# Norms: GpSimd adds squared tiles in pairs, and TensorE sums the pairs with ones

## The reference

```python
def layer_norm(x, g, b):
    mu = jnp.mean(xf, axis=-1, keepdims=True)
    var = jnp.mean(jnp.square(xf - mu), axis=-1, keepdims=True)
    y = (xf - mu) * lax.rsqrt(var + LN_EPS) * g + b

# and, without centring,
y = x * lax.rsqrt(jnp.mean(x * x, axis=-1, keepdims=True) + eps) * w
```

## Time and profile before

| what | value |
|---|---|
| median of 3 runs | 4329.05 us (4323.47 to 4330.01) |
| the profiled execution | 4340.69 us, its span 4338.9 us |
| TensorE busy | 3790.5 us, 87% of the span, 19109 matmuls |
| VectorE busy | 2528.5 us, 58% |
| ScalarE busy | 1207.0 us, 28% |
| GpSimd busy | 348.2 us, 8%, 276 instructions |
| granted TensorE clock, mean | 0.93 |
| sums of squares (L153) on TensorE | 176 matmul records |
| squares (L166) on ScalarE | 88 |

### The profile page before, as it was taken

The page is one execution under the profiler, slowest core; times in us unless marked ns, Lnnn a source line. Parts: engine busy times, 40 slices in busy tenths (PEclk is TensorE's granted clock), DMA queues, the critical chain, the costliest instruction groups (busy, mean ns, idle before and its releaser), DMA issues. The chain is left out here.

```text
span 4338.9 us, 51551 instructions
## 1 busy us (share of the span) xinstructions
PE 3790.5 (87%) x19109; PEld 3261.0 (75%) x19109; DVE 2528.5 (58%) x4080; ACT 1207.0 (28%) x2101; POOL 348.2 (8%) x276
## 2 busy tenths in 40 slices
PE   7998977799986988889999979999877879779998
PEld 6876764478755787689999979999856848566876
DVE  4544778454434563369999867777643436654433
ACT  1101122121012232233578833333221122412300
POOL 0000011000000020002212212222100000000000
PEclk9999978799998989999999989999988979889999
DMA  3222710222211001238889889998612101021232
GB/s 140 97 71 82 255 60 1 95 74 96 73 64 58 29 1 40 87 119 271 293 291 330 307 302 329 324 336 314 220 58 73 51 33 67 1 78 68 87 104 71
DMA packets 198386, 590.94 MB, mean 136 GB/s; under 512 B 22448, under 2 KB 80688, under 8 KB 196016
## 3 DMA queue, kind: packets, MB, share of 16 engines
q1 hardware_dynamic: 161344, 454.38, 30.3%
q0 software_dynamic: 36864, 134.23, 8.7%
HBM read 536.11 MB, written 52.43 MB: 136 GB/s over the span
## 5 line engine op out<-in xcount | busy, mean ns | idle before, releaser
L350 DVE CAST w_hi<-w_ring 128x1024 fp32r<-128x1024 f32 (+1 forms) x336 | 238.5, 710 | 644.0 <-PE banks L315 495.8
L71 DVE TENSOR_TENSOR w_lo<-w_ring,w_hi 128x1024 fp32r<-128x1024 f32 (+1 forms) x336 | 424.5, 1263 | 11.5
L315 PE MATMUL banks<-x_hi,w_hi 128*128 128x512 f32 x896 | 355.8, 397 | 46.9 <-DVE x_lo L71 46.8
L2385 PE MATMUL out_ps<-w_hi,v_hi 128*128 128x384 f32 x1024 | 349.2, 341 | 45.5 <-DVE w_lo L71 45.5
L2085 PE MATMUL up_ps<-h_hi,u_hi 128*128 128x384 f32 x1024 | 351.4, 343 | 21.2 <-DVE u_lo L71 21.2
L315 PE MATMUL banks<-x_lo,w_hi 128*128 128x512 f32 x896 | 354.4, 396 | 0.0
L315 PE MATMUL banks<-x_hi,w_lo 128*128 128x512 f32 x896 | 354.2, 395 | 0.0
L2385 PE MATMUL out_ps<-w_hi,v_lo 128*128 128x384 f32 x1024 | 347.6, 339 | 0.0
L2385 PE MATMUL out_ps<-w_lo,v_hi 128*128 128x384 f32 x1024 | 347.6, 339 | 0.0
L2085 PE MATMUL up_ps<-h_lo,u_hi 128*128 128x384 f32 x1024 | 343.8, 336 | 0.0
L2085 PE MATMUL up_ps<-h_hi,u_lo 128*128 128x384 f32 x1024 | 343.6, 336 | 0.0
(11 more groups left out here) (532 smaller groups left out, 7812.0 us busy)
## 6 DMA issues: line engine op xcount, KB each, us to landing
expert_tiles<-peer_u SPq DMA_DIRECT2D x128, 512.0 KB
expert_tiles<-peer_v SPq DMA_DIRECT2D x128, 512.0 KB
w_ring<-w_in SPq DMA_DIRECT2D x104, 512.0 KB, 3.6
w_ring<-ffn_up SPq DMA_DIRECT2D x88, 512.0 KB, 3.5
w_ring<-w_ff SPq DMA_DIRECT2D x64, 512.0 KB, 3.8
ada_ring<-w_ada SPq DMA_DIRECT2D x48, 512.0 KB, 5.2
peer_acts<-act_ring SPq DMA_DIRECT2D x128, 192.0 KB
peer_gates<-staging SPq DMA_DIRECT2D x12, 2048.0 KB
```

The source lines that it names most:

```text
L71: return nc.vector.tensor_tensor(self.lo[at], value, self.hi[at].bitcast(F32), ALU.subtract)
L315: last = nc.tensor.matmul(banks[:, j, s, 0:n], a[:, u % 2, k, :], b[:, g * kg + k, x_from + c:x_from + c + n], start=(g == 0 and k == 0 an ...
L350: nc.vector.tensor_copy(w_parts.hi[:, u % 2], ring[:, u % slots]).then_inc(hi_ready, 1)
L2385: last = nc.tensor.matmul(out_ps[:, b, P:T], a[:, n % 2, b * P:b * P + P], r[:, n % 2, :], start=(n == 0 and part == 0), stop=(n == NKEYS ...
```

## The change

Where a norm has at least four slots, GpSimd adds the squares of tiles 2i and 2i+1 into the slot of the former, as soon as both are there. TensorE waits for that sum and multiplies it with ones, so a norm of eight tiles has four summed tiles, and one of four tiles has two. ScalarE's wait for a free slot is now for the summed pair: squares 4 and 5 wait for pair 0, squares 6 and 7 for pair 1. The norm with two slots stays as it was. All stage classes get a GpSimd part, `run` and `linear` play it, and each of these norms takes one more semaphore. One clearing of semaphores, with its barrier, is added in the second block, ahead of the projection "out2".

```diff
--- before.py
+++ after.py
@@ -87,6 +87,9 @@
     def tensor(self, pe):
         pass
 
+    def gpsimd(self, pool):
+        pass
+
     def scalar(self, act):
         for k in range(self.kb):
             self.p.nc.scalar.activation(self.parts.hi[:, k, :], self.src[:, k, :], ACT.Copy).then_inc(self.hi_ready, 1)
@@ -115,6 +118,9 @@
         self.sq = p.sb(ctx, "squares", [P, 4, width])[:] if squares is None else squares
         self.rstd = p.sb(ctx, "rstd", [P, width])[:] if rstd is None else rstd
         self.slots = self.sq.shape[1]
+        self.paired = self.slots >= 4
+        self.sums_of = kb // 2 if self.paired else kb
+        (self.pair_ready,) = p.sems(ctx, "pair_ready") if self.paired else (None,)
         self.dst = dst
         self.eps_col = p.sb(ctx, "eps_col", [P, 1])
         self.sums = p.ps(ctx, "sums", [P, 2 if center else 1, halves, 512])
@@ -147,12 +153,24 @@
                     last = nc.tensor.matmul(self.sums[:, 0, j, 0:n], self.p.ones, self.src[:, k, c:c + n],
                                             start=(k == 0), stop=(k == kb - 1))
             last.then_inc(self.mean_ready, 1)
-        for k in range(kb):
-            pe.wait_ge(self.sq_ready, k + 1)
+        for i in range(self.sums_of):
+            if self.paired:
+                pe.wait_ge(self.pair_ready, i + 1)
+            else:
+                pe.wait_ge(self.sq_ready, i + 1)
+            at = (2 * i if self.paired else i) % self.slots
             for j, (c, n) in enumerate(self.spans):
                 last = nc.tensor.matmul(self.sums[:, 1 if self.center else 0, j, 0:n], self.p.ones,
-                                        self.sq[:, k % self.slots, c:c + n], start=(k == 0), stop=(k == kb - 1))
+                                        self.sq[:, at, c:c + n], start=(i == 0), stop=(i == self.sums_of - 1))
             last.then_inc(self.sq_used, 1)
+
+    def gpsimd(self, pool):
+        if self.paired:
+            for i in range(self.sums_of):
+                at = 2 * i % self.slots
+                pool.wait_ge(self.sq_ready, 2 * i + 2)
+                self.p.nc.gpsimd.tensor_tensor(self.sq[:, at, :], self.sq[:, at, :], self.sq[:, at + 1, :], ALU.add) \
+                    .then_inc(self.pair_ready, 1)
 
     def scalar(self, act):
         nc, kb, center = self.p.nc, self.kb, self.center
@@ -162,11 +180,11 @@
             else:
                 self.source_ready(act, k)
             if k >= self.slots:
-                act.wait_ge(self.sq_used, k - self.slots + 1)
+                act.wait_ge(self.sq_used, (k - self.slots) // 2 + 1 if self.paired else k - self.slots + 1)
             nc.scalar.activation(self.sq[:, k % self.slots, :], (self.dst if center else self.src)[:, k, :], ACT.Square) \
                 .then_inc(self.sq_ready, 1)
         act.wait_ge(self.eps_set, 1)
-        act.wait_ge(self.sq_used, kb)
+        act.wait_ge(self.sq_used, self.sums_of)
         nc.scalar.activation(self.halved(self.rstd), self.total(1 if center else 0), ACT.Sqrt, bias=self.eps_col[:],
                              scale=1.0 / (kb * P)).then_inc(self.rms_ready, 1)
         for k in range(kb):
@@ -214,6 +232,9 @@
     def __init__(self, landed, count):
         self.landed, self.count = landed, count
 
+    def gpsimd(self, pool):
+        pool.wait_ge(self.landed, 16 * self.count)
+
     def tensor(self, pe):
         pe.wait_ge(self.landed, 16 * self.count)
 
@@ -238,6 +259,11 @@
         def _(act):
             for stage in stages:
                 stage.scalar(act)
+
+        @block.gpsimd
+        def _(pool):
+            for stage in stages:
+                stage.gpsimd(pool)
 
         @block.vector
         def _(dve):
@@ -297,6 +323,11 @@
                 with sp.Fori(0, bodies - 1) as i:
                     body(i, False)
             body(bodies - 1, True)
+
+        @block.gpsimd
+        def _(pool):
+            for stage in front:
+                stage.gpsimd(pool)
 
         @block.tensor
         def _(pe):
@@ -1124,6 +1155,7 @@
             mix = p.sb(c, "mix", [P, DB, T])
             mixer2(p, x, mix, ln3, gains[:, 0, :], sh1, gm_norm, o_norm)
             mix_parts = Parts(p, c, "mix", [P, DB, T])
+            p.clear_semaphores()
             linear(p, "out2", d["w_out2"], DB, DB, mix_parts, dve_out=residual_out(p, x, gt1),
                    stages=lambda c2: [Split(p, c2, mix, mix_parts, DB)])
         p.clear_semaphores()
```

## The result

The change makes the kernel slower: 4345.96 us in the median of 8 runs (4338.21 to 4353.44) against 4330.81 of the kernel before (8 runs, 4319.48 to 4337.83) on the same chip, ratio 1.0039 with a 95% interval of 1.0027 to 1.0052, so 12 to 23 us. The forecast was 4341 in a range of 4326 to 4355. The two profiled executions lie only 4.7 us apart, where the forecast had 4352.4 for the later one. Executions differ by more than that outside of the norms, so what follows compares the norms one by one and takes the total from the medians.

The account below looks back on a forecast made before the run. Eleven serial norm windows that nothing covers were taken as the bound, TensorE's matmuls setting the pace inside. 6.6 + 0.3 + 2.2 + 1.2 + 0.6 + 0.85 = 11.75 us on the 4329.05 median gave 4341, range 4326 to 4355.

Parts of the forecast that it names:

- The price of an add: GpSimd's addition of two tiles of squares takes 1.21 us, bounds 1.14 and 1.36.
- The schedule: Long norm, square 4 waiting for pair 0's sum: 8.6 us at full clock against 7.90 before, 11.1 at half.
- The clock, warm norms: Three norms formerly at full clock: a 3.3 us pause before the first sum lowers it, 10.1 us each, +6.6 in all.
- Cold norms: Five norms starting at half clock: full clock returns late or never, 10.6 us each, together +0.3, bounds -2.2 and +2.8.
- the meeting at 1750: GpSimd's adds 1 and 2 coincide with VectorE's weight splits, one waiting out the other: +1.2 us, bounds 0 and 2.4.
- Short norms: Two norms of four tiles: 5.6 us against 4.49, together +2.2, bounds +0.8 and +3.8.
- The narrow norm: Norm of the meta tokens' sixteen columns, at 3144: adds meet VectorE's splits, +0.6 us, bounds 0 to 2.
- The clearing: New barrier ahead of the second mixer's output projection delays its weight fetch: +0.85 us, bounds 0.3 and 1.4.
- The first rival: Full clock survives the 3.3 us pause in at least two of three warm norms: about +3.4 us, 4332; chance 0.3.
- the second: Rival: sums spaced by adds keep TensorE at half clock in every norm, +19 us, 4348; chance 0.2.

Follow-up runs that it names:

- the change once more: The changed kernel unaltered, run again for a second profile and more runs: 4347.59 us, ratio 1.0042 to the kernel before.
- clearing alone: The kernel before with only the added clearing of semaphores ahead of the second mixer's output projection: 4329.11 us, ratio 1.0008.
- fillers: The changed kernel with matmuls of constants, results overwritten, ahead of the first pair's sum in five norms: 4333.68 us, ratio 1.0021 to the kernel before.
- adds twice: The changed kernel with a second GpSimd addition of the same size behind each: 4378.65 us, ratio 1.0123 to the kernel before.
- eight slots: The changed kernel with eight slots in place of four for the squares in six long norms: 4331.03 us, ratio 1.0000 to the kernel before.
- sums one by one: The kernel before, with VectorE adding each square to the first in four norms and TensorE summing one tile: 4326.91 us, ratio 1.0001.
- keep warm: The kernel before, with matmuls of constants, results overwritten, ahead of the sums in four norms that start at half clock: 4320.69 us, ratio 0.9980.
- warm, pairs on VectorE: The kernel before with constant matmuls ahead of sums in five norms; in four, VectorE adds the pairs, with six slots: 4312.83 us, ratio 0.9960.

## Why the prediction held

The kernels can be put in one table. The middle column is the sum of the eleven windows less the 89.4 of before, with 1.4 us for the clearing where it is in; the last is what was timed.

| kernel | windows and clearing | as a ratio | measured ratio |
|---|---|---|---|
| the change | +12.6 | 1.0029 | 1.0039 |
| the change once more | +14.2 | 1.0033 | 1.0042 |
| clearing alone | +1.3 | 1.0003 | 1.0008 |
| fillers | +8.1 | 1.0019 | 1.0021 |
| adds twice | +54.4 | 1.0126 | 1.0123 |
| eight slots | +3.2 | 1.0007 | 1.0000 |
| sums one by one | -4.4 | 0.9990 | 1.0001 |
| keep warm | -10.7 | 0.9975 | 0.9980 |
| warm, pairs on VectorE | -17.3 | 0.9960 | 0.9960 |

Each measured ratio is within 0.11% of its windows, and each interval holds the ratio of the windows: from -17 to +54 us, what a norm gains or loses comes out in the time. Nothing covers a norm, which was the ground the forecast stood on.

Step by step, with the two profiles of the change:

- **The price of an add**: 1.21 us forecast from GpSimd's own rows, 1.27 measured. The ratio of 2 to VectorE of the Trainium skill (GPSIMD Engine Reference, section Engine selection) gave an estimate of 1.36; against VectorE's 0.69 us the measured ratio is 1.84. The page's advice, VectorE for such an add, fits the last experiment, which also had the slots and the warm clock.
- **The schedule**: 8.6 us at full clock forecast, 8.83 at 1.00 measured. The slot wait that it names (square 4 behind pair 0) is in the timeline, and eight slots take it away.
- **The clock, warm norms**: +6.6 forecast, +7.4 and +7.9 measured. The pause was 3.40 us (3.3 forecast). The size was right, the course in part luck. The forecast took half clock at first and full clock for the last pair, 10.1 us, and no warm norm did that. Two ran all sums at half clock (11.22 and 11.09, the 11.1 of the schedule), one none (8.83, its 8.6), and three began at full clock and fell during the second pair (10.36 to 10.65), a case that the forecast did not have. That the mean of the six, 10.5, lies near 10.1 is owed to the mixture of these cases and not to the one that was forecast.
- **Cold norms and the meeting at 1750**: +0.3 and +1.2 forecast, together -0.3 and +0.8 measured. Here the mixed case is found, if with two pairs at full clock at the end: 10.26, 10.08 and 10.19 us, and 11.12 where all stayed at half. Which norm came back varied between the profiles (3151 and 3172 had 11.01 and 10.94 in the second), so the forecast's middle holds for the group only. The meeting is there, at 0.7 and 1.0 us of adds instead of 1.2.
- **Short norms**: +2.2 forecast, +3.5 in both profiles. The step that failed in size is the middle of 4.9 and 6.4: both short norms came out nearer to the cold end or past it, with 5.96 to 6.54.
- **The narrow norm**: +0.6 forecast, +0.7 measured.
- **The clearing**: +0.85 forecast, +1.36 measured, its upper bound. The comparison took another place, which has 1.34 us with a clearing where this one has 1.85 and 1.88; why isn't shown. The same place with and without the line gives the price.

In sum 11.75 forecast, 12.6 and 14.2 found in the profiles, 15 and 17 in the medians. The terms that were too small (warm norms, short norms, clearing: 2.6 and 3.1 us) and those that were too large (cold norms and meeting: 1.8 and 0.7 us) cancel in part. The bounds as they were added give 4327 to 4354, and the range was stated 1 us wider on each side; that decides nothing here. The first rival, a warm clock, happened in one of six warm windows, and not in two of three, as it would have had to; the second, half clock everywhere, in none of the two profiles as a whole.

## What to carry to other kernels

Taking work off the busiest engine can cost time where that work lies in a serial passage: count the chain from the first input to the last consumer, with every hand-off and every buffer that must come free, not the engine's sum. Combining tiles two by two also doubles the grain at which buffers come free, so it wants more slots. And look at what a pause does to TensorE's clock before and after it: here the clock was worth 3 us in a passage of 8, more than the whole idea of the pairs.

## What the runs showed of the hardware that was not expected

- The length of TensorE's pause alone did not decide the clock: after 3.40 us ahead of the first sum the window at 1269 had 1.00 (8.83 us) in one execution of the same kernel and 0.69 (10.62 us) in another. And the clock need not fall within the pause: in the second it was 1.00 through the pause and the first pair, and 0.50 from the third pair on.
- Matmuls on constants whose result is overwritten held the clock as real ones do: three windows of 10.27 to 10.90 us came to 7.90 and 7.91 at 1.00.
- A 128x16 add on GpSimd took 0.30 us undisturbed and 0.66 to 1.30 us beside VectorE's weight splits, a 128x512 add 1.27 us undisturbed and 1.36 to 2.18 beside them: the wait does not shrink with the add.
- Dependent additions on VectorE through one tile stand 0.80 us apart, where eight independent operations of the same shape (the subtraction of the mean in the earlier trace rows, 4.87 us) follow at 0.60.
